# Expert weights landed in twelve 1 MB halves instead of six 2 MB pieces, in a float32 decoder layer

## The reference

```
logits = (xt @ w_router) + b_router
top_val, top_idx = lax.top_k(logits, 4)          # 4 of 32 experts for each token
gates = softmax(top_val)
# for each expert e that has tokens:
hh  = xb @ w_gu[e] + b_gu[e]                     # 1024 -> 2048 (gate half, linear half)
glu = minimum(hh[:, :1024], 7.0)
lin = clip(hh[:, 1024:], -7.0, 7.0)
act = glu * sigmoid(1.702 * glu) * (lin + 1.0)
out[tokens of e] += (act @ w_down[e] + b_down[e]) * gate
```

## Time and profile before

| | |
|---|---|
| median of 3 runs | 1302.39 us (1299.95 to 1303.49) |
| the profiled execution | 1300.58 us, of which the profile's span is 1298.8 us |
| TensorE | 1228.1 us busy (95%) |
| VectorE, ScalarE | 273.1 us (21%), 219.7 us (17%) |
| read from HBM | 433.57 MB, mean 335 GB/s over the span |
| expert weights issued in the loop | 186 of 2048 KB |

### The profile page before, as it was taken

The page is one execution under the profiler, slowest core; times in us unless marked ns, Lnnn a source line. Parts: engine busy times, 40 slices in busy tenths (PEclk is TensorE's granted clock), DMA queues, the critical chain, the costliest instruction groups (busy, mean ns, idle before and its releaser), DMA issues.

```text
span 1298.8 us, 17995 instructions
## 1 busy us (share of the span) xinstructions
PE 1228.1 (95%) x7532; PEld 613.2 (47%) x7532; DVE 273.1 (21%) x592; ACT 219.7 (17%) x342; POOL 0.2 (0%) x4
## 2 busy tenths in 40 slices
PE   6999996897999999999999999999999999999997
PEld 5888765645344444444333443333333443333333
DVE  2534443333111111111111111111111111111122
ACT  2511422212011111111111111111111111111023
POOL 0000000000000000000000000000000000000000
PEclk9999997695999999999999999999999999999999
DMA  9631120162799999999999999999999999999930
GB/s 384 259 130 66 56 77 1 37 238 103 294 427 430 428 428 428 428 429 429 428 428 428 428 429 428 428 428 429 429 428 428 429 428 429 428 428 428 428 154 33
DMA packets 31981, 435.07 MB, mean 335 GB/s; under 512 B 3952, under 2 KB 4080, under 8 KB 5456
## 3 DMA queue, kind: packets, MB, share of 16 engines
q1 hardware_dynamic: 31952, 434.63, 79.4%
HBM read 433.57 MB, written 1.05 MB: 335 GB/s over the span
## 4 chain that ended last, share of the span: by engine, by line
PE 50%; DMA 43%; DVE 3%; ACT 2%; issue 1%; SPq 0%; DVEq 0%; ACTq 0%
DMA ring<-in_we 43%; PE PS L719 22%; PE PS L420 6%; PE PS L462 3%; PE PS L691 3%; PE PS L788 2%; PE PS L606 2%; PE PS L700 2%; PE PS L557 1%; PE PS L740 1%; PE PS L432 1%; PE PS L425 1%; PE PS L534 1%; DVE B L1012 1%; PE PS L679 1%
## 5 line engine op out<-in xcount | busy, mean ns | idle before, releaser
L719 PE MATMUL PS<-ring,FV 128*64 128x512 f32 x3072 | 680.3, 596 | 21.2 <-DMA ring<-in_we 21.2
L719 PEld LDWEIGHTS PS<-ring,FV 128*64 128x64 f32 x3072 | 213.1, 137 | 461.6 <-issue 410.1
L691 PE MATMUL PS<-rz,B 128*128 128x64 f32 x1024 | 121.3, 278 | 0.0
L691 PEld LDWEIGHTS PS<-rz,B 128*128 128x128 f32 x1024 | 120.1, 196 | 1.5 <-issue 1.5
L1294 DVE TENSOR_SCALAR rz<-con,lora 64x64 f32<-64x64 f32 x32 | 7.9, 246 | 437.9 <-PE PS L719 437.9
L420 PE MATMUL PS<-hT,ring 128*128 128x256 f32 x416 | 93.0, 382 | 0.9 <-ACT hT L818 0.9
L420 PEld LDWEIGHTS PS<-hT,ring 128*128 128x128 f32 x416 | 78.1, 190 | 12.5 <-ACT hT L818 1.2
L949 ACT ACTIVATE FV<-PS 128x512 f32<-128x512 f32 x32 | 19.1, 597 | 280.5 <-PE PS L754 280.5
L700 PE MATMUL PS<-B,rz 64*128 64x512 f32 x264 | 65.6, 615 | 0.0
L947 ACT ACTIVATE hT<-hT 128x512 f32<-128x512 f32 x32 | 20.1, 629 | 235.8 <-DVE hT L1311 235.8
L1315 DVE TENSOR_SCALAR hT<-PS 128x512 f32<-128x512 f32 x32 | 22.1, 691 | 170.5 <-PE PS L719 170.5
(11 more groups left out here) (244 smaller groups left out, 693.7 us busy)
## 6 DMA issues: line engine op xcount, KB each, us to landing
ring<-in_we SPq DMA_DIRECT2D x192, 2048.0 KB, 22.0
ring<-in_wz SPq DMA_DIRECT2D x7, 2048.0 KB, 22.3
ring<-in_wo SPq DMA_DIRECT2D x2, 2048.0 KB, 8.1
B<-in_wgate SPq DMA_DIRECT2D x2, 2048.0 KB, 9.8
con<-in_con SPq DMA_DIRECT2D x1, 1181.0 KB, 7.3
xq<-in_x SPq DMA_DIRECT2D x2, 512.0 KB, 4.6
ring<-in_wz SPq DMA_DIRECT2D x1, 1024.0 KB, 9.5
xq<-in_x SPq DMA_DIRECT2D x1, 1024.0 KB, 7.0
```

Source lines behind the costliest of these rows:

```text
L691: mm = pe.matmul(PS[:, 6, k * SLOTS:(k + 1) * SLOTS], H2[:, b, k * P:(k + 1) * P], PM[:, b, :], start=(b == 0), stop=(b == TB - 1))
L719: mm = pe.matmul(PS[64 * h:64 * h + 64, bank_, :], lhs(4 * (q % 2) + k), w[:, k, h, :], start=(first and k == 0), stop=(q % 2 == 1 and k = ...
```

## The change

`ring` keeps its size and place, but is now used as twelve halves of 1 MB, `half(u)`: half u is one half of slot u // 2. The weights in HBM are laid out as twelve blocks of 1 MB for each expert, each 128 rows of 8 KB. Each half has its own transfer, its own semaphore `s_half[u]`, its own wait on TensorE and its own rise of `s_used`. The products, their operands and their order are the same; the counts for which VectorE, ScalarE and SyncE wait are doubled. The pieces of the first part (`wz`, `wo`) land in the slots as before.

```
+        def half(u):
+            return ring[:, u // 2, (u % 2) * 2048:(u % 2) * 2048 + 2048]
...
             def first_item(q):
-                sp.dma_start(ring[:, q, :], t["we"][0, q]).then_inc(s_slot[q], 16)
+                for u in (2 * q, 2 * q + 1):
+                    sp.dma_start(half(u), t["we"][0, u]).then_inc(s_half[u], 16)
...
-                for q in range(6):
-
-                    sp.wait_ge(s_used, 6 * i + (q + 1))
-                    sp.dma_start(ring[:, q, :], t["we"][bass.ds(e, 1), q, :, :].rearrange("a p n -> (a p) n"))\
-                        .then_inc(s_slot[q], 16)
+                for u in range(2 * NSLOT):
+
+                    sp.wait_ge(s_used, 12 * i + (u + 1))
+                    sp.dma_start(half(u), t["we"][bass.ds(e, 1), u, :, :].rearrange("a p n -> (a p) n"))\
+                        .then_inc(s_half[u], 16)
...
             def product(i, q, bank_, lhs, first):
-                w = ring[:, q, :].rearrange("p (k h c) -> p k h c", k=4, h=2)
-                pe.wait_ge(s_slot[q], 16 * i + 16 * (LANDED[q] + 1))
-                for k in range(4):
-                    for h in range(2):
-                        mm = pe.matmul(PS[64 * h:64 * h + 64, bank_, :], lhs(4 * (q % 2) + k), w[:, k, h, :],
-                                       start=(first and k == 0), stop=(q % 2 == 1 and k == 3))
-                mm.then_inc(s_used, 1)
+                for u in (2 * q, 2 * q + 1):
+                    w = half(u).rearrange("p (k h c) -> p k h c", k=2, h=2)
+                    pe.wait_ge(s_half[u], 16 * i + 16)
+                    for k in range(2):
+                        for h in range(2):
+                            mm = pe.matmul(PS[64 * h:64 * h + 64, bank_, :], lhs(2 * (u % 4) + k), w[:, k, h, :],
+                                           start=(first and u % 4 == 0 and k == 0), stop=(u % 4 == 3 and k == 1))
+                    mm.then_inc(s_used, 1)
...
-                act.wait_ge(s_used, 6 * i + 6)
+                act.wait_ge(s_used, 12 * i + 12)
...
-                v.wait_ge(s_used, 6 * i + 2)
+                v.wait_ge(s_used, 12 * i + 4)
...
-    gu = a["w_gu"][0].reshape(NE, 2, 4, P, 2, FF).transpose(0, 4, 1, 3, 2, 5).reshape(NE, 4, P, 4 * FF)
-    dn = a["w_down"][0].reshape(NE, 2, 4, P, D).transpose(0, 1, 3, 2, 4).reshape(NE, 2, P, 4 * D)
+    gu = a["w_gu"][0].reshape(NE, 4, 2, P, 2, FF).transpose(0, 4, 1, 3, 2, 5).reshape(NE, 8, P, 2 * FF)
+    dn = a["w_down"][0].reshape(NE, 4, 2, P, D).transpose(0, 1, 3, 2, 4).reshape(NE, 4, P, 2 * D)
```

More of the change, by code:

```diff
@@ L247, in fox_rwkv7_moe_ple @@
         s_slot = [sem(f"slot{i}_landed") for i in range(NSLOT)]
+        s_half = [sem(f"half_piece{i}_landed") for i in range(2 * NSLOT)]
         s_bd = sem("b_down_landed")
@@ L710, in project @@
                 return mm
-            LANDED = (2, 2, 1, 1, 2, 2)
             def product(i, q, bank_, lhs, first):
-                w = ring[:, q, :].rearrange("p (k h c) -> p k h c", k=4, h=2)
-                pe.wait_ge(s_slot[q], 16 * i + 16 * (LANDED[q] + 1))
-                for k in range(4):
-                    for h in range(2):
-                        mm = pe.matmul(PS[64 * h:64 * h + 64, bank_, :], lhs(4 * (q % 2) + k), w[:, k, h, :],
-                                       start=(first and k == 0), stop=(q % 2 == 1 and k == 3))
-                mm.then_inc(s_used, 1)
+                for u in (2 * q, 2 * q + 1):
[6 more added lines that the diff above has]
+                    mm.then_inc(s_used, 1)
             def x_of(k):
@@ L1313, in item @@
                 tt(e_s, e_g, e_s, ALU.mult)
-                v.wait_ge(s_used, 6 * i + 4)
+                v.wait_ge(s_used, 12 * i + 8)
                 v.tensor_scalar(e_l, bank(7), LIMIT, -LIMIT, ALU.min, ALU.max).then_inc(s_vl, 1)
```

## The result

The changed kernel takes 1311.55 us (median of 20 runs, 1309.48 to 1316.63) against 1302.55 (20 runs, 1297.27 to 1309.91): 9.0 us more, ratio 1.007, 95% interval 1.0056 to 1.0083. The forecast was 1311, slower. The profiled execution took 1312.39 us with a span of 1310.6, that is 11.8 us more span than the profile before.

The account below looks back on a forecast made before the run. The prediction took the DMA engines, full with weight transfers, as the bound. Stream 13.1 us longer, less 1.8 at the start and 1.8 at the end, made 9.5 us more: 1311 us, with 1300 to 1317 for 8 in 10.

Parts of the forecast that it names:

- The DMA bounds the loop, by its packets: Expert loop: full DMA engines bound it at 427 to 430 GB/s; each packet's own cost lies on the path.
- The stream: Loop's weight transfers: 9 more packets per engine per 2 MB at 8 ns each, 13.1 us lost over 182 transfers.
- The start: Loop's first transfers: earlier release of half pieces starts the stream sooner, 1.8 us gained, bounds 0 and 2.3.
- The end: Last item: only half of piece 3 remains after its last byte lands, 1.8 us gained, bounds 1.0 and 3.6.
- The sum: Whole kernel: 13.1 - 1.8 - 1.8 = 9.5 us slower, forecast time 1311 us.
- SyncE: Weight issues in the loop: twice as many stay hidden; even if slowed to 1.8 us each, the DMA stays full.
- The share of DMA in the chain: Profile of the changed kernel: DMA's share of the chain stays high.
- TensorE's waits on `ring`: Loop: waits grow from 21.2 us to 30 or more, as the item's period goes from 29.37 to 29.8 us.
- rival 1: Loop stream: packet cost overlaps almost wholly, only the two gains remain, 1297.0 or 1298.8 us; chance 0.17.
- rival 2: Loop stream: packet cost is the low 4 ns, +3.0 us, 1303.6 to 1305.4 us; chance 0.16.
- rival 3: Packet cost is 15 ns, or the extra is also felt in the first part: +21 us, 1322 to 1324; chance 0.05.
- Rival 4: Last item: the gain fails because the slower stream binds at piece 5, +11 us, 1313; chance 0.05.

Follow-up runs that it names:

- e1: Kernel before with only the HBM layout changed to rows of 8 KB; the six 2 MB transfers, waits and releases unchanged: 1315.76 us against 1303.4, ratio 1.0093.
- e2: Kernel before with each 2 MB piece in two 1 MB transfers, even and odd partitions, rows still 16 KB, release per piece: 1299.25 us, ratio 0.9974.
- e3: The change carried further: 24 transfers of 512 KB per item with 4 KB rows, each with its own semaphore, wait and release: 1338.2 us, ratio 1.0276.
- e4: Kernel before with only the loop's first turn issued in halves, TensorE raising its count per half: 1302.8 us, ratio 1.0012; second set 1303.0, 1.0014.
- e5: Kernel before with only piece 3 of the last item landing in two halves with their own semaphores: 1301.61 us, ratio 0.9996.
- after: The changed kernel, all pieces in halves of 1 MB with 8 KB rows, against the kernel before: 1311.55 us against 1302.55, ratio 1.007.
- e8: Kernel before with 4 MB transfers of 32 KB rows in all loop turns but the first and last, which go in halves: 1298.86 us, ratio 0.9971.
- e9: e8 with turns 1 to 4 of the loop in pieces of 2 MB and 4 MB pairs from turn 5 on: 1298.02 us, ratio 0.9971 against before.
- e7: Kernel before with three 4 MB transfers per item, 32 KB rows, each issued when both its pieces are used: 1301.85 us, ratio 0.999.

## Why the prediction was right

- **The DMA bounds the loop, by its packets.** Right. The share is above 100% and the rate follows the size of the packets in all six kernels of the table; transfers and semaphores do not matter (e1 against e2).
- **The stream: 9 packets x 8 ns = 72 ns per 2 MB, 13.1 us.** The mechanism was right and the sum close: 13.9 us in the profile, and 12.9 in e1, where the rows alone are changed. Its two parts were each a little off, and the two errors nearly cancel. A data packet costs 9.4 ns and a 4 B packet about nothing, so it is 8 x 9.4 = 75. The price itself was partly luck: the short stretches of the earlier trace rows gave 4, 8.7 and 15 ns from mixed small packets, and the one chosen happened to be near. The estimate from the Trainium skill's 4 KB stream, 9 ns, was nearer still, and e3 now has that row size in a long stream: 410 GB/s, against the 408.7 of the Trainium skill (DMA: Bandwidth & Descriptors, the section on the iDMA fabric). The Trainium skill (DMA: Bandwidth & Descriptors, the section on the anatomy of one DMA) calls the bubble of the semaphore write about one cycle; e2 agrees, within what its rows can tell.
- **The start, -1.8 us.** S to I fell by 1.8 as worked out, and the first issue came 3.8 us after S in place of 5.9, 2.1 against the 2.3 forecast. It came at 331.7 and not at 330, for the first item itself began 1.4 us later, and so did the issue for piece 4, at 352.16 and not at 350.8. What failed is "from here on the stream never stops": from 354 to 358 us the changed kernel ran at 340 and 352 GB/s only. From 24 to 32 us after S it moved 3.02 MB, against 3.34 MB in the first profile of e4, so some 0.8 us of the gain is lost again (an estimate: 0.32 MB at 422 GB/s; both have rows of 8 KB there). That loss stands inside I to L: 899.3 and 898.6 us, against 898.2 in e1, which has the same data packets. And e4 says that, won alone, this gain is not seen in the time.
- **The end, -1.8 us.** -1.7 measured. A single item in halves gave 1.2 (e5), so the full gain needs the items before it in halves too, as the prediction's "over one or two items" had it.
- **Both ends together** are what after has over e1: 3.4 us when each is set against the kernel before of its own set of runs (+12.4 and +9.0 us), 2.4 us in S to E of the profiles (927.9 against 925.5), 3.6 by the prediction.
- **The sum.** Forecast +9.5, measured +9.0 in the medians and +10.4 and +9.8 from S to E in two profiles. That the median hit 1311 within 1 us is finer than the terms deserve: it is within the scatter.
- **SyncE.** The guess that issues would be held came true and was too small: up to 3.4 us, not 1.8. That it costs the stream nothing was right, here and at twice the count in e3.
- **The share of DMA in the chain** was to stay high, and this sign failed: 23% in place of 43%. The chain now passes through TensorE's products and SyncE's held issues, with the DMA engines as full as before. The bound was read rightly from the engines' share and the rate; the chain's shares did not bear on it.
- **TensorE's waits on `ring`** were to grow from 21.2 to 30 us or more. They grew to 23.5 in 600 to 1250 us only; over the whole run the wait shows at the weight loads instead, 86.5 us against 49.2. The item's period did grow, from 29.37 to 29.82 us (654.84 to 714.47 in the chain is two items), as forecast. This sign failed as it was written, but the term behind it held.
- **Rivals.** By the prediction's own prices, the loop would run at 428 GB/s by rival 1 (packets overlap), about 425 by rival 2 (4 ns) and about 416 by rival 3 (15 ns). It ran at 422. Rival 4 (piece 5 binds at the end) falls by the chain: the 32 records of pieces 4 and 5 take 7.02 us there, as before, without a wait.

## What to carry to other kernels

When the DMA engines are full, count packets, not transfers: this weight stream goes faster with longer rows, and each split of a row is paid in full. A transfer that is cut between its rows costs nothing (e2); one that is cut through its rows does (the change, and e1 with no more transfers than before). What finer pieces can win lies at the two ends of the stream and is bounded by one piece's work there, so try them at the ends and nowhere else, and keep the release fine until the queue has become long. Expect little: e8 and e9 are 0.3% faster than the kernel before, and an earlier release alone (e4) brought nothing.

## What the runs showed of the hardware that was not expected

- A row of 32 KB is a single packet (7907 data packets for 259.10 MB in e7), and 9.4 ns per packet holds from 4 to 32 KB.
- SyncE's issue is held when the queue is deep. In after the longest took 3.4 us, with a transfer of the chain landing 26.46 us after its issue, or 10.7 halves of 2.48 us; in e3 it is about 12 quarters (15.78 us by 1.28). e2, with 24.7 us at most (10.1 transfers of 1024 KB), has no issue over 0.52 us, and e1, with 25.95 us (5.2 transfers), none over 0.41. This would fit a limit on transfers a little above 10. It fits a limit on packets as well: with its 4 B packets an engine has 9 per transfer in after and e3, so some 96 and 111 under way; 17 in e1 and 5 in e2, so some 88 and 50. No run tells the two apart.
- In the second profile of e4 the last piece landed late: TensorE had waited 2.21 us, and the granted clock fell to 0.50, the lower of its two levels (1.2 GHz), while TensorE worked on that piece.

```profile
1237.16 5.28 PE L726 MATMUL PS<-ring,FV 128*64 128x512 f32 x16 [2.21 <-DMA ring<-in_we]
```
```profile
1238.00:1240.00 2.00, 2.00 (x8) 0.68 (x6) 0.00 (x0) 0.00 (x0) 0.00 (x0) 0.50 0.95 401
```

  16 records took 5.28 us in place of 3.65. In the other profiles the products waited at most 1.3 us at a time from 345 to 1240 us, and the granted clock was 1.00 in every window of 5 us from 345 to 1235 us.
- The first part's length scatters, with S from 325.1 to 331.6 us over all the profiles. In e8, the latest, the granted clock of 200 to 260 us was 0.59; before it was 0.66. In the records of the kernel before that were taken with the experiments (73 executions), the mean granted clock and the time go together: 1297.0 to 1299.6 us at 0.970 to 0.972 (14 of them), 1303.4 to 1309.1 us at 0.964 and below (25). TensorE's clock in the first part is thus likely why times of one kernel spread over some 10 us; no run tested it. At a mean clock of 0.968 alone, e4 has medians of 1301.7 and 1301.4 us against 1302.0 and 1301.1 before, so the spread does not hide its missing gain.
